# Six weight slots instead of four in the first stage of a hybrid trunk layer, with x loaded at once and PE's order rewritten

## The chip, the cores and the metric

One NeuronCore of one Trainium2 chip runs the whole layer as one program. The metric is the device time of one execution in microseconds (us). Times inside the profile count from the start of the profiled span. Engines are named as in the profile: PE is TensorE (PEld its weight loads), ACT ScalarE, DVE VectorE, POOL GpSimd and SP SyncE; "q" behind a name is the engine's sequencer, which issues DMAs.

## The reference

One inference step of a one-layer diffusion trunk in float32: 512 latent tokens and 128 context tokens, model width 2048. Only the beginning matters here:

```python
mod = silu(cvec) @ w_mod + b_mod                       # for c and c_ctx; w_mod is 2048 x 12288
sh1, sc1, g1, sh2, sc2, g2 = split(mod, 6)
h = rmsnorm(x, g_pre1) * (1 + sc1) + sh1
proj = h @ w_in
xr, gr, q, k, v, gates = split(proj, ...)              # v has 1024 columns
...
```

After that come a bidirectional recurrent branch, differential attention, an output projection and a mixture of 16 experts. The outputs are both token sets, the new key and value caches and the recurrent state.

## The kernel before

The program is written by hand: each engine has one list of instructions, and semaphores tie the lists together. Every float32 weight is split into a high and a low part (ACT writes `w_hi`, DVE `w_lo`), and a product is three matmuls, low x high, high x low, high x high (`three`, lines 540 to 544).

**The first stage** computes shift and scale (the first 4096 columns of `w_mod`), normalises and transposes x, and begins the values v with `w_in`. Its weights come in units of 1 MiB, each two DMAs of 512 KB on SP's queue (line 592) into one of four slots of `raw`. `START` (lines 69 to 73) lists the units: 32 units `("mod", m)` of `w_mod` and four units `("v", h)` of `w_in`. In this text unit i is the one at place i of the list, from 0. Before, v0 to v3 are units 8, 13, 22 and 31, and mod 31 is unit 35. Four more units for the second half of the values follow as units 36 to 39. `start_load` (line 583) issues unit i into slot i % 4 when the unit four places earlier has been used: a mod unit by PE (`start_used`), a v unit by DVE's low split (`lo_ready`). SP's list is in order, so a load that waits holds back all behind it.

**PE's list** (lines 2309 to 2393) is an order written out by hand from these pieces:
- `mod_unit(m)` (L2282): four matmuls of one unit against the columns of silu(c). Units 4s to 4s + 3 make row s; rows 0, 2, 4, 6 are shift quarters, rows 1, 3, 5, 7 scale quarters.
- `turn_x(t)` (L2271): 16 matmuls that transpose and scale tile t of x (five tiles of 128 tokens) into PSUM banks 4 to 7. It waits for the diagonal of 1/rms that DVE makes (`norm_diagonal`) from ACT's sum of squares (`square`), and for the copies of tile t - 1 out of the same banks (`take_x`, two by ACT, two by DVE).
- `turn_rows(s)` (L2295): turns row s, which ACT has copied from PSUM (`row_out`, L1047), into columns.
- `turn_parameters` (L2299): turns small parameter rows into PSUM.
- `first_values(k)` (L542 to L544): 15 matmuls of the first 512 value columns for block k of the model width. It needs `tokens(k)` and, for k = 0, 4, 8, 12, the split v unit. With `amid=s` a `turn_rows(s)` stands inside, behind six of the 15 matmuls.

**ACT and DVE** work h = 0 to 3 in order: split v unit h (for h = 0 ahead of the loop), copy or add rows 2h and 2h + 1 (`row_out`, `mod_columns`), then `tokens` for four blocks: ACT scales, shifts and takes the high part (L1037, L1040), DVE the low part (L1517). `tokens` of group h need A1 (L1511), which DVE writes after `turn_rows(2h + 1)`. So ACT splits v unit h only behind the tokens of group h - 1 (lines 1064 to 1072, 1543 to 1553):

```python
for h in range(4):
    if h:
        v_split_hi(act, h, 0); v_split_hi(act, h, 1)
        row_out(2 * h); row_out(2 * h + 1)
    act.wait_ge(S["a1_ready"], h + 1)
    for k in range(4 * h, 4 * h + 4):
        tokens(k)
```

After the last group ACT and DVE split unit 36, DVE computes a softplus in a dozen short steps (lines 1564 to 1592) and copies the values out of PSUM (`take_values`, L1541); PE's next stage, `wide(Q_V + 1, ...)`, waits for those copies.

**x** is loaded by ACT's own queue (`load_x`, L1016): tiles 0 and 1 behind silu(c), tile t + 2 behind `square(t)`. Small parameter rows come on POOL's queue. `mod_raw` (three slots of 8 KB a partition) is used only in the stage behind, where DVE computes the other modulation columns; before that its first slot holds `c2` and `sel2`, its third the diagonals.

Of the kernel before, what the change touches and what calls it, by code (L numbers as in the profile page):

```python
# [22 lines left out]
P = 128  # L23
D = 2048
# [25 lines left out]
NSLOT = 8  # L50
UNITS = 24
QUADS = [8, 2, 8, 8, 4, 8, NE * 6]
# [20 lines left out]
assert all(i % NRAW == m for m, i in V_AT.items()) and len(START) == (Q_V + 1) * NRAW  # L73
# [41 lines left out]
def trunk(nc, a, out_ctx, out_lat, out_k, out_v, out_state):  # L115
    ctx = ExitStack()
    with ctx:
# [42 lines left out]
        def place(at0, items):  # L160

            o, made = at0, {}
            for name, shape, dt in items:
# [21 lines left out]
        A["diag"] = at("diag", [P, 2, P], F32, mod_at + 2 * UB + 256)  # L185
# [246 lines left out]
        def f_loaded(t):  # L432

            j = (F_UNIT + t) % NSLOT
            return raw_loaded[j], (Q_EXP * INC if j < NRAW else 0) + (UNITS // NSLOT * NE + 1) * 16

# [9 lines left out]
        def exp_loads(e, k):  # L446

            return (Q_EXP * INC if k % NSLOT < NRAW else 0) + (UNITS // NSLOT * e + k // NSLOT + 1) * 16

# [22 lines left out]

        def start_loaded(eng, i):

            eng.wait_ge(raw_loaded[i % NRAW], (i // NRAW + 1) * INC)
# [86 lines left out]
        def _(sp):  # L562
# [7 lines left out]
            def wide(w, j, kq, c0):  # L570

                v = raw[:, j, :].rearrange("p (k n) -> p k n", k=4)
# [10 lines left out]
            def start_load(i, parts):  # L583

                if i >= NRAW:
                    what, n = START[i - NRAW]
# [4 lines left out]
                for dst, src in parts:  # L591
                    sp.dma_start(dst, src).then_inc(raw_loaded[i % NRAW], INC // 2)

            for i, (what, n) in enumerate(START):
                if what == "mod":
                    start_load(i, wide(w_mod, i % NRAW, n % 4, n // 4 % 2 * D + n // 8 * 512))
# [402 lines left out]
        def _(act):  # L999
# [6 lines left out]
            act.dma_start(ident[:], a["ident"]).then_inc(S["c_loaded"], 16)  # L1006
            act.wait_ge(S["const_set"], 1)
# [6 lines left out]
            def load_x(t):  # L1014
                src = a["x_sample"][0][t * P:(t + 1) * P, :] if t < TT - 1 else a["x_prompt"][0]
                act.dma_start(x_in[:, t, :], src).then_inc(x_loaded[t % 2], 16)  # L1016

            def square(t):

                act.wait_ge(x_loaded[t % 2], (t // 2 + 1) * 16)  # L1020
# [1845 lines left out]
```

## Time and profile before

| | us |
|---|---|
| median of 3 runs | 2847.84 |
| lowest, highest | 2847.01, 2848.12 |
| the profiled execution | 2848.99 |
| its span | 2847.4 |

A profile shows one execution. Rows with "busy" give the time in which an engine had an instruction running; matmuls overlap, so a busy PE need not be at its peak. A wait names the engine and the line whose work ended last before the waiting instruction went on. "DMA share" is the mean busy share of the core's 16 DMA engines (it can exceed 1, as packets overlap), GB/s what they moved, PEclk the granted clock of TensorE as a share of 2.4 GHz. q1 is SP's DMA queue, q10 ACT's, q0 POOL's.

### The profile page before, as it was taken

The page shows a single profiled execution, that of the slowest core. Times are in us where ns is not written, and L with a number is a line of the kernel's source. Part 1 is how long each engine was busy: PE and PEld are TensorE (multiplying, and loading weights), DVE is VectorE, ACT ScalarE, POOL GpSimd, SP SyncE. Part 2 cuts the span into 40 slices and gives each one's busy share as a digit, 9 for nine tenths or more (in the row PEclk, how much of TensorE's full clock was granted, in tenths as well). Part 3 has the DMA queues.
Part 4 walks back from the last instruction along what each step waited for, and adds up shares of the span by engine and source line. Part 5 has one row for each costly group of instructions (what it writes and reads, how often), then busy time and mean ns, then how long its engine had stood idle before and what let it go on. Part 6 is the DMA issues. An engine that isn't in the chain of part 4 may idle for free.

```text
span 2847.4 us, 40931 instructions
## 1 busy us (share of the span) xinstructions
PE 2791.4 (98%) x15008; PEld 2390.7 (84%) x15008; DVE 2106.8 (74%) x1918; ACT 1502.7 (53%) x1466; POOL 282.0 (10%) x337
## 2 busy tenths in 40 slices
PE   7999999999999999999999997999999999999998
PEld 5688888899999999999988776888888888888886
DVE  2339788796777777763344577888888888888888
ACT  4411221125556566552233455777777777777776
POOL 1000000002111111100000001001010101100100
PEclk9999999999999999999999997999999999999999
DMA  9877667664343443364343767999999999999997
GB/s 370 311 266 255 228 252 265 224 227 135 120 123 119 123 123 123 102 207 124 123 143 119 292 215 276 356 402 395 395 398 389 396 393 397 391 388 387 392 394 297
DMA packets 258406, 757.23 MB, mean 266 GB/s; under 512 B 20249, under 2 KB 127297, under 8 KB 194001
## 3 DMA queue, kind: packets, MB, share of 16 engines
q1 hardware_dynamic: 234272, 650.01, 61.3%
q0 software_dynamic: 23120, 100.71, 10.9%
q10 hardware_dynamic: 928, 5.33, 0.5%
q8 instruction: 59, 0.97, 0.1%
q14 instruction: 27, 0.21, 0.0%
HBM read 700.61 MB, written 55.37 MB: 265 GB/s over the span
## 4 chain that ended last, share of the span: by engine, by line
PE 91%; DVE 3%; DMA 2%; ACT 1%; issue 1%; DVEq 0%; ACTq 0%; SPq 0%; POOL 0%; POOLq 0%
PE ps L542 21%; PE ps L544 21%; PE ps L543 21%; PE ps L2402 5%; PE ps L2403 5%; PE ps L2404 5%; PE ps L2569 3%; PE ps L2571 3%; PE ps L2570 3%; PE ps L2259 2%; PE ps L2507 1%; DMA raw<-in_w_mod 1%; DVE rsd L1827 1%; PE ps L2282 1%; DVE xc L1649 0%
## 5 line engine op out<-in xcount | busy, mean ns | idle before, releaser
L467 DVE TENSOR_TENSOR we_lo<-raw,we_hi 128x2048 fp32r<-128x2048 f32 x384 | 877.5, 2290 | 114.0 <-ACT we_hi L462 113.8
L462 ACT ACTIVATE we_hi<-raw 128x2048 fp32r<-128x2048 f32 x384 | 736.9, 1920 | 261.4 <-PE ps L544 261.4
L411 ACT ACTIVATE w_hi<-raw 128x2048 fp32r<-128x2048 f32 x115 | 220.1, 1914 | 444.3 <-PE ps L544 356.5
L421 DVE TENSOR_TENSOR w_lo<-raw,w_hi 128x2048 fp32r<-128x2048 f32 x115 | 263.5, 2291 | 192.4 <-ACT w_hi L411 187.8
L542 PE MATMUL ps<-we_hi,xs_lo 128*128 128x512 f32 x1024 | 399.7, 390 | 0.1
L544 PE MATMUL ps<-we_hi,xs_hi 128*128 128x512 f32 x1024 | 399.3, 390 | 0.0
L543 PE MATMUL ps<-we_lo,xs_hi 128*128 128x512 f32 x1024 | 399.3, 390 | 0.0
L2402 PE MATMUL ps<-hi,w_lo 128*128 128x320 f32 x1152 | 365.3, 317 | 0.9 <-ACT stage L1122 0.9
L2403 PE MATMUL ps<-lo,w_hi 128*128 128x320 f32 x1152 | 355.9, 309 | 0.0
L2404 PE MATMUL ps<-hi,w_hi 128*128 128x320 f32 x1152 | 355.8, 309 | 0.0
L1614 DVE SCALAR_TENSOR_TENSOR mod_acc<-mod_raw,sc,mod_acc 128x2048 f32<-128x2048 f32 x120 | 276.7, 2348 | 3.3
L542 PEld LDWEIGHTS ps<-we_hi,xs_lo 128*128 128x128 f32 x1024 | 192.8, 188 | 41.9 <-issue 0.7
L544 PEld LDWEIGHTS ps<-we_hi,xs_hi 128*128 128x128 f32 x1024 | 192.8, 188 | 40.2
L543 PEld LDWEIGHTS ps<-we_lo,xs_hi 128*128 128x128 f32 x1024 | 192.8, 188 | 39.4
L2402 PEld LDWEIGHTS ps<-hi,w_lo 128*128 128x128 f32 x1152 | 216.3, 188 | 9.8 <-issue 8.9
L2403 PEld LDWEIGHTS ps<-lo,w_hi 128*128 128x128 f32 x1152 | 216.6, 188 | 0.0
L2404 PEld LDWEIGHTS ps<-hi,w_hi 128*128 128x128 f32 x1152 | 216.3, 188 | 0.0
L542 PE MATMUL ps<-we_hi,hid_lo 128*128 128x512 f32 x512 | 201.3, 393 | 0.4 <-DVE hid_lo L2166 0.4
L544 PE MATMUL ps<-we_hi,hid_hi 128*128 128x512 f32 x512 | 199.5, 390 | 0.0
L543 PE MATMUL ps<-we_lo,hid_hi 128*128 128x512 f32 x512 | 199.3, 389 | 0.0
L542 PE MATMUL ps<-hi,w_lo 128*128 128x512 f32 x448 | 175.2, 391 | 0.0
L544 PE MATMUL ps<-hi,w_hi 128*128 128x512 f32 x448 | 174.5, 389 | 0.0
(447 smaller groups left out, 4772.0 us busy)
## 6 DMA issues: line engine op xcount, KB each, us to landing
raw<-in_w_e_gate SPq DMA_DIRECT2D x128, 1024.0 KB, 8.0
raw<-in_w_e_up SPq DMA_DIRECT2D x128, 1024.0 KB, 7.5
raw<-in_w_e_down SPq DMA_DIRECT2D x128, 1024.0 KB, 12.1
raw<-in_w_in SPq DMA_DIRECT2D x144, 512.0 KB, 5.7
mod_raw<-in_w_mod SPq DMA_DIRECT2D x64, 1024.0 KB, 5.3
raw<-in_w_mod SPq DMA_DIRECT2D x64, 512.0 KB, 7.6
raw<-in_w_o SPq DMA_DIRECT2D x64, 512.0 KB, 4.9
d_proj<-g_stage POOLq DMA_DIRECT2D x32, 320.0 KB, 2.4
```

The source lines that it names most:

```text
L411: act.activation(w_hi[:, j % NHL, s], raw[:, slot, s], ACT.Copy).then_inc(hi_ready, 1 if fine else 2)
L421: dve.tensor_tensor(w_lo[:, j % NHL, s], raw[:, slot, s], w_hi[:, j % NHL, s].bitcast(F32), ALU.subtract).then_inc(lo_ready, 1 if fine else 2)
L462: act.activation(we_hi[:, k % NEH, :], raw_slot(k), ACT.Copy).then_inc(hi_ready, 2)
L467: TTn(we_lo[:, k % NEH, :], raw_slot(k), we_hi[:, k % NEH, :].bitcast(F32), ALU.subtract).then_inc(lo_ready, 2)
L542: pe.matmul(out, s_lo, m_hi, start=start, stop=False)
L543: pe.matmul(out, s_hi, m_lo, start=False, stop=False)
L544: return pe.matmul(out, s_hi, m_hi, start=False, stop=stop)
L1614: last = STT(mod_acc[:, v, :], w, c, mod_acc[:, v, :], ALU.mult, ALU.add)
L2402: pe.matmul(out, wl, hi[:, k, ms], start=(k % 16 == 0), stop=False)
L2403: pe.matmul(out, wh, lo[:, k, ms], start=False, stop=False)
L2404: last = pe.matmul(out, wh, hi[:, k, ms], start=False, stop=(k == KT - 1))
L2569: pe.matmul(out, wl, hi[:, k, ms], start=(kk == 0), stop=False)
```

## The change

The first stage gets six slots: the four of `raw` and the second and third of `mod_raw` (`first_slot`), whose diagonals move to a spare tile. `START` becomes one list with v0 to v3 at places 6, 13, 20 and 27, so that each lies in slot h; `start_load` waits for the unit six places earlier. ACT issues all five tiles of x right behind the constants, each on a semaphore of its own (three are shared with later loads, whose targets rise by 16), and loads the table for Sqrt early. ACT, DVE and PE get new orders: PE starts with `turn_x(0)` and alternates it with units; `turn_rows(3)`, `(5)` and `(7)` no longer stand inside a `first_values`; `turn_parameters` writes to bank 3; `take_x` of all tiles now precedes the column copies on DVE and `row_out(0)` on ACT. `loads_ahead` replaces the count of earlier loads that the experts' slots expect.

```diff
@@ constants and START
+NFIRST = 6
-QUADS = [8, 2, 8, 8, 4, 8, NE * 6]
+QUADS = [5, 2, 8, 8, 4, 8, NE * 6]
-START = [("mod", m) for m in range(8)] + [("v", 0)] + [x for h in range(1, 4) for x in [
-    ("mod", 8 * h + m) for m in range(4)] + [("v", h)] + [("mod", 8 * h + m) for m in range(4, 8)]]
+V_PLACE = (6, 13, 20, 27)
+_mods = iter(range(32))
+START = [("v", V_PLACE.index(i)) if i in V_PLACE else ("mod", next(_mods)) for i in range(36)]
@@ SBUF
-        A["diag"] = at("diag", [P, 2, P], F32, mod_at + 2 * UB + 256)
+        A["diag"] = at("diag", [P, 2, P], F32, PLACED["spare"])
@@ semaphores and slots
+        x_sems = x_loaded + [S["g2_loaded"], S["vec_lat_loaded"], S["rope_loaded"]]
+        def first_slot(i):
+            j = i % NFIRST
+            return raw[:, j, :] if j < NRAW else mod_raw[:, j - NRAW + 1, :]
         def start_loaded(eng, i):
-            eng.wait_ge(raw_loaded[i % NRAW], (i // NRAW + 1) * INC)
+            eng.wait_ge(raw_loaded[i % NFIRST], (i // NFIRST + 1) * INC)
+        def loads_ahead(j):
+            return Q_EXP * INC if j < NRAW else (Q_V + 1) * INC if j < NFIRST else 0
@@ SP
             def start_load(i, parts):
-                if i >= NRAW:
-                    what, n = START[i - NRAW]
+                if i >= NFIRST:
+                    what, n = START[i - NFIRST]
...
-                    sp.dma_start(dst, src).then_inc(raw_loaded[i % NRAW], INC // 2)
+                    sp.dma_start(dst, src).then_inc(raw_loaded[i % NFIRST], INC // 2)
@@ ACT
             act.dma_start(ident[:], a["ident"]).then_inc(S["c_loaded"], 16)
+            for t in range(TT):
+                src = a["x_sample"][0][t * P:(t + 1) * P, :] if t < TT - 1 else a["x_prompt"][0]
+                act.dma_start(x_in[:, t, :], src).then_inc(x_sems[t], 16)
...
+            act.activation(misc[:, 6:7], eps_col, ACT.Sqrt)
...
-            load_x(0)
-            load_x(1)
             for t in range(TT):
                 square(t)
-                if t + 2 < TT:
-                    load_x(t + 2)
-                if t:
-                    take_x(t - 1)
+                if t >= 2:
+                    take_x(t - 2)
+            take_x(TT - 2)
+            take_x(TT - 1)
             row_out(0)
             v_split_hi(act, 0, 0)
             row_out(1)
             v_split_hi(act, 0, 1)
-            take_x(TT - 1)
@@ DVE
-            dve.wait_ge(S["rows_turned"], 2)
-            own.done(dve.tensor_copy(A["cols_b"][:], ps[:, 4, 0:48]))
-            own.done(dve.tensor_copy(A["cols2"][:], ps[:, 5, 0:105]))
-            own.settle()
             for t in range(TT):
                 norm_diagonal(t)
                 if t:
                     take_x(t - 1)
+            take_x(TT - 1)
+            dve.wait_ge(S["rows_turned"], 2)
+            own.done(dve.tensor_copy(A["cols_b"][:], ps[:, 3, 0:48]))
+            own.done(dve.tensor_copy(A["cols2"][:], ps[:, 3, 64:169]))
+            own.settle()
+            mod_columns(0)
             v_split_lo(dve, 0, 0)
-            mod_columns(0)
+            mod_columns(1)
             v_split_lo(dve, 0, 1)
-            take_x(TT - 1)
-            mod_columns(1)
@@ PE
             pe.wait_ge(S["c_ready"], 1)
+            turn_x(0)
             mod_unit(0)
+            turn_x(1)
             mod_unit(1)
+            turn_x(2)
+            mod_unit(2)
+            mod_unit(3)
+            turn_x(3)
             turn_parameters()
-            for m in range(2, 8):
-                mod_unit(m)
-                if m == 7:
-                    turn_rows(0)
-                if m >= 3:
-                    turn_x(m - 3)
+            mod_unit(4)
+            turn_x(4)
+            mod_unit(5)
+            mod_unit(6)
+            turn_rows(0)
+            mod_unit(7)
+            pe.wait_ge(S["xt_act"], 2 * TT)
+            pe.wait_ge(S["xt_dve"], 2 * TT)
+            mod_unit(8)
             turn_rows(1)
...
-            mod_units(8, 11)
+            mod_units(9, 11)
             first_values(0)
+            first_values(1)
             mod_units(11, 12)
-            first_values(1)
-            mod_units(12, 13)
             first_values(2)
+            mod_units(12, 14)
             turn_rows(2)
-            mod_units(13, 16)
-            first_values(3, amid=3)
-            mod_units(16, 18)
+            mod_units(14, 16)
+            first_values(3)
+            mod_units(16, 17)
+            turn_rows(3)
+            mod_units(17, 18)
             first_values(4)
-            mod_units(18, 20)
+            mod_units(18, 21)
             first_values(5)
-            mod_units(20, 21)
+            mod_units(21, 22)
+            turn_rows(4)
+            mod_units(22, 24)
             first_values(6)
-            turn_rows(4)
-            mod_units(21, 24)
-            first_values(7, amid=5)
-            mod_units(24, 26)
+            turn_rows(5)
+            first_values(7)
+            mod_units(24, 27)
             first_values(8)
-            mod_units(26, 28)
             first_values(9)
-            mod_units(28, 30)
             first_values(10)
+            mod_units(27, 30)
             turn_rows(6)
             mod_units(30, 32)
-            first_values(11, amid=7)
+            first_values(11)
+            turn_rows(7)
             for k in range(12, KT):
                 first_values(k)
```

## Rows read from the trace of the kernel before

**Rows 1.** Busy time by stretch; engines, then PEclk, DMA share, GB/s.
```profile
0.00:10.50 10.50, 0.31 (x1) 0.18 (x1) 2.11 (x9) 1.72 (x3) 8.61 (x18) 1.00 0.82 283
15.50:20.40 4.90, 0.00 (x0) 0.00 (x0) 0.00 (x0) 3.44 (x4) 0.00 (x0) 0.68 1.01 401
20.40:121.60 101.20, 96.99 (x628) 63.64 (x629) 30.11 (x50) 49.29 (x75) 0.00 (x0) 0.98 1.04 383
139.70:260.00 120.30, 120.29 (x533) 99.59 (x534) 70.97 (x40) 20.08 (x15) 6.30 (x10) 1.00 0.69 255
```

**Rows 2.** Waits of PE and SP's queue, 0 to 140: total, times, longest.
```profile
PE ps L2282 <- DMA raw<-in_w_mod: 8.9, 6, 5.0
...
SPq L592 <- PE ps L2282: 64.0, 21, 7.1
...
SPq L592 <- DVE w_lo L487: 11.3, 4, 3.8
```

**Rows 3.** The chain, 0 to 260: start, us, what.
```profile
38.01 3.77 PE ps L2271 x32
...
47.43 0.80 PE ps L2295 x8
...
55.30 0.99 PE ps L2282 x8
...
59.93 1.00 PE ps L2282 x8
...
95.65 0.79 PE ps L2295 x8
...
120.84 0.80 PE ps L2295 x8
...
139.71 0.47 PE ps L542
```

**Rows 4.** DMA queues from 13 to 19 us: packets, MB, share.
```profile
q10 hardware_dynamic: 258, 1.98, 80.0%
q1 hardware_dynamic: 256, 0.49, 21.8%
```

**Rows 5.** Timeline of ACT and its queue: x0's issue, its first square.
```profile
9.05 0.84 ACTq L1016 DMA_DIRECT2D x_in<-in_x_sample  x2
...
16.94 1.91 ACT L1022 ACTIVATE junk<-x_in 128x2048 f32<-128x2048 f32 x1 [7.74 <-DMA x_in<-in_x_sample]
```

**Rows 6.** Timeline of PE: the first turn_x.
```profile
22.31 4.65 PE L2271 MATMUL ps<-diag,x_in 128*128 128x128 f32 x32
```

**Rows 7.** Busy time by stretch again; DMA share and GB/s stand last.
```profile
66.00:74.00 8.00, 8.00 (x59) 4.43 (x51) 1.16 (x3) 3.67 (x7) 0.00 (x0) 1.00 0.95 315
100.00:103.00 3.00, 3.00 (x19) 2.14 (x12) 1.22 (x2) 2.97 (x5) 0.00 (x0) 1.00 1.05 365
103.00:117.00 14.00, 12.73 (x73) 7.53 (x72) 3.62 (x4) 3.90 (x6) 0.00 (x0) 1.00 1.05 387
```

**Rows 8.** Timeline of SP's queue: three units' issues.
```profile
46.09 0.89 SPq L592 DMA_DIRECT2D raw<-in_w_mod  x2
...
109.96 0.88 SPq L592 DMA_DIRECT2D raw<-in_w_mod  x2
...
133.87 0.88 SPq L567 DMA_DIRECT2D raw<-in_w_in  x2
```

**Rows 9.** DMA issues at 109.96 and 133.87: KB each, median us to landing.
```profile
raw<-in_w_mod SPq DMA_DIRECT2D x2, 512.0 KB, 6.1
...
raw<-in_w_in SPq DMA_DIRECT2D x2, 512.0 KB, 4.4
```

**Rows 10.** Timelines of ACT and DVE: tokens 8 to 11, then v3's split.
```profile
96.87 1.20 ACT L1037 ACTIVATE xT<-xT,cols,A 128x512 f32<-128x512 f32 x2 [2.15 <-DVE A L1511]
...
103.70 0.74 ACT L1040 ACTIVATE hi<-xT 128x640 fp32r<-128x640 f32 x1
...
106.48 2.01 ACT L481 ACTIVATE w_hi<-raw 128x1024 fp32r<-128x1024 f32 x2 [2.04 <-DMA raw<-in_w_in]
...
107.57 2.36 DVE L487 TENSOR_TENSOR w_lo<-raw,w_hi 128x1024 fp32r<-128x1024 f32 x2 [2.28 <-ACT w_hi L481]
```

More of the change, by code:

```diff
@@ L66 @@
 MOD_FROM = [sum(MOD_TILES[:n]) for n in range(8)]
-START = [("mod", m) for m in range(8)] + [("v", 0)] + [x for h in range(1, 4) for x in [
-    ("mod", 8 * h + m) for m in range(4)] + [("v", h)] + [("mod", 8 * h + m) for m in range(4, 8)]]
+V_PLACE = (6, 13, 20, 27)
+_mods = iter(range(32))
+START = [("v", V_PLACE.index(i)) if i in V_PLACE else ("mod", next(_mods)) for i in range(36)]
 MOD_AT = {m: i for i, (what, m) in enumerate(START) if what == "mod"}
 V_AT = {m: i for i, (what, m) in enumerate(START) if what == "v"}
-assert all(i % NRAW == m for m, i in V_AT.items()) and len(START) == (Q_V + 1) * NRAW
+assert all(i % NFIRST == m for m, i in V_AT.items()) and len(START) == (Q_V + 1) * NFIRST
 ORDER = (4, 2, 3, 0, 1)
@@ L591, in start_load @@
                 for dst, src in parts:
-                    sp.dma_start(dst, src).then_inc(raw_loaded[i % NRAW], INC // 2)
+                    sp.dma_start(dst, src).then_inc(raw_loaded[i % NFIRST], INC // 2)
             for i, (what, n) in enumerate(START):
                 if what == "mod":
-                    start_load(i, wide(w_mod, i % NRAW, n % 4, n // 4 % 2 * D + n // 8 * 512))
+                    start_load(i, wide(w_mod, i % NFIRST, n % 4, n // 4 % 2 * D + n // 8 * 512))
                 else:
@@ L2055, in _ @@
                 if c == 0:
-                    dve.wait_ge(S["vec_lat_loaded"], 32)
+                    dve.wait_ge(S["vec_lat_loaded"], 48)
                 if c == 2:
@@ L2215, in _ @@
             expert(NE - 1, 1, True)
-            dve.wait_ge(S["g2_loaded"], 32)
+            dve.wait_ge(S["g2_loaded"], 48)
             def gain(i, t):
@@ L2282, in mod_unit @@
                     last = pe.matmul(ps[32 * kk:32 * kk + 32, bank, :], c2[:, 4 * kp + kk, :],
-                                     raw[:, i % NRAW, kk * 512:kk * 512 + 512], start=(kp == 0), stop=(kp == 3))
+                                     first_slot(i)[:, kk * 512:kk * 512 + 512], start=(kp == 0), stop=(kp == 3))
                 last.then_inc(S["start_used"], 1)
@@ L2300, in turn_parameters @@
                 pe.wait_ge(par_loaded, N_PAR * 16)
-                turn(ps[:, 4, 0:48], A["rows3"][:], 48)
-                turn(ps[:, 5, 0:105], A["rows2"][:], 105).then_inc(S["rows_turned"], 1)
+                turn(ps[:, 3, 0:48], A["rows3"][:], 48)
+                turn(ps[:, 3, 64:169], A["rows2"][:], 105).then_inc(S["rows_turned"], 1)
             def spread_lambda():
@@ L2340, in wide, with first_values @@
                     last.then_inc(halves_used, 2)
-            def first_values(k, amid=None):
+            def first_values(k):
                 kq, s = k // 4, slice(k % 4 * 512, k % 4 * 512 + 512)
@@ L2353, in first_values @@
                         last.then_inc(S["bank_done"], 1)
-                    if amid is not None and t == 1:
-                        turn_rows(amid)
                 if k % 4 == 3:
```

15 lines of the change are left out of this document (5 added, 10 removed).

## Prediction

> **What bounds the kernel now.** The page comes first: PE is busy nearly throughout, and the change touches only the first 5% of the span. The table by stretch shows what that part can pay [rows 1]: from 139.7 us on PE has no gap (120.29 of 120.30 us), so only the moment counts at which it enters that stage. Ahead of it PE stands still for 4.9 us (15.5 to 20.4), and from 20.4 to 121.6 us it is busy for 96.99 of 101.20 us while the DMA share is 1.04. Both limits lie on top of each other. The waits say how [rows 2]: PE waited 8.9 us for w_mod, but SyncE stood 64.0 us in front of a slot that PE had not released and 11.3 us in front of one that VectorE's low split had not. With four slots the transfers run on PE's releases and PE on the transfers. The chain runs accordingly through pieces of PE and pieces of w_mod up to the last turn_rows (L2295), which ends at 120.84 + 0.80 = 121.6 us [rows 3].
>
> Behind that turn_rows the order is fixed and the same in both kernels: VectorE writes A1, ScalarE and VectorE make tokens 12 to 15, split the next unit, walk the softplus chain and copy v_stage, and PE enters the next stage at 139.7, 18.1 us after turn_rows(7) ended [rows 3]. I call that end R7. **The change moves the end of the kernel by what it moves R7**, as nothing later is edited but semaphore targets that count x's tiles in.
>
> **x's five tiles at once.** Queue shares are read from 13 to 19 us [rows 4]: ScalarE's queue took 1.98 MB and SyncE's 0.49 MB, four to one. x0 was issued at 9.05 and squared from 16.94 [rows 5], 7.9 us. Issued behind the constants at about 2.5 it lands near 10.4; the tiles behind it follow 3.2 us apart (1.05 MB at 1.98 MB per 6 us), x2 near 16.8. Total bytes are unchanged, so for the last weights this part is worth nothing: the same queues carry 41 MiB. The early Sqrt costs nothing, its table load falls into the wait for x0, 7.74 us long before [rows 5]; the five issues (0.4 us each) lie where ScalarE waited for cols_ready.
>
> **PE up to turn_rows(1).** PE now starts with turn_x(0), which needs x0 squared (2.1 us), rooted and put on the diagonal (0.9): 13.5 us instead of 10.5. turn_x(0) took 4.65 us in the stretch after a stand of 4.9 us with a granted clock of 0.68, that is partly at 1.2 instead of 2.4 GHz [rows 1, 6]; warm ones take 3.77 [rows 3]. I take 4.65, since PE starts from a stand here too, with 3.77 and 5.5 (another such surcharge) as ends. Then mod_unit(0) 1.0; turn_x(1) waits for ScalarE's copy, which is now queued behind square(2): 16.8 + 2.4 + 0.6 = 19.8; four more turn_x 15.1, six units 5.7, the parameters 0.4, turn_rows(0) 0.9: 41.9; mod_unit(7) to 42.9. mod_unit(8) is the tenth unit, so 15 MiB with x: 2.8 us of start (10.5 us at 283 instead of 387 GB/s, [rows 1]) plus 15 x 2.71 us (1 MiB at 387 GB/s, [rows 7]) plus 0.6 to report, 44.0. It ends at 44.9, turn_rows(1) at **45.8**. Before, it ended at 48.2 [rows 3], so 2.4 us are won here.
>
> **Six slots, and who holds them.** Releases by PE are no longer late: after 45.8 us every ordinary unit is asked for over 5 us ahead. But SyncE's queue is in order, and units 12, 19, 26 and 33 each wait until VectorE has split the V unit six places earlier. Two of these are late.
> Unit 12 waits for v0's second half, which now stands behind mod_columns(1): 45.8 + 0.4 + 1.2 = 47.4, when unit 11 is almost through. The old unit 12 was issued at 46.09 [rows 8], so the lead is gone here. On an empty queue a unit is home 5.2 us after its first issue (133.87, median 4.4 us, the second half later, [rows 8, 9]); with work ahead it took 7.0 (109.96 and 6.1, [rows 8, 9]). Restarting a dry queue costs extra: 1.5 us in 66 to 74 us (315 instead of 387 GB/s), 0.2 us in 100 to 103 [rows 7]; I take 0.8, between them. Unit 12 lands at 53.4.
> From there 14 units at 2.71 bring mod 23 (unit 26) at 91.3. Its slot is free in time: mod 15 lands at 66.9, turn_rows(3) ends 6.4 later (a unit, first_values(3), a unit, the turn) and v2 is split 11.4 behind that, at 84.7, when unit 25 is still 3.9 us from home. Mod 23 takes 0.9, first_values(6) 3.6 (4.63 for a unit and a first_values between 55.30 and 59.93, [rows 3]), turn_rows(5) 0.9: that ends at **96.8**, called R5; before 96.4 [rows 3].
> Unit 33 waits for v3, which ScalarE may split only behind tokens 8 to 11. From R5: A1 0.4, tokens 7.6 (96.87 to 104.44), split 2.0, VectorE's last half 1.4 behind it [rows 10]: 11.4, so 108.2. The units up to 32 are home at 91.3 + 6 x 2.71 = 107.6: the queue is dry again. Unit 33 lands 5.2 + 0.8 later, mod 31 two units on, 119.6 (before: about 117.1, by the issue at 109.96). Old v3 was the 32nd unit and blocked one load; new v3 is the 28th and blocks three.
>
> **The tail.** first_values(11) now stands whole (3.6) ahead of turn_rows(7), where six of its fifteen products did: mod 31 0.9 + 3.6 + 0.9 = 5.5. R7 = 119.6 + 5.5 = **125.1** against 121.6: **+3.5 us**. PE alone, never waiting, would need 27.3 from R5 (five first_values 18.2, eight units 7.3, two turn_rows 1.8): 124.1, one microsecond less, so the transfer decides. Behind R7 PE has nothing left to do until tokens 12 are there, 3.2 us, but VectorE's chain of 18.1 us is as long as before and covers it. In one line R7 = R5 + 28.3. Parameters in bank 3, the moved column copies (0.5 us) and the moved diagonal lie ahead of turn_rows(0) and cost nothing while x's copies take longer.
>
> The sum is made against the profiled execution, 2848.99 us with a span of 2847.4; the median of the three runs shown is 2847.84, so +3.5 gives **2851.3 us**. Without restart costs it is +1.9, with 1.5 us for each +4.9; the clock of turn_x(0) adds 0.9 either way: +1.0 to +5.8.
>
> The pace of 387 GB/s is that of 103 to 117 us [rows 7]. The Trainium skill (DMA: Bandwidth & Descriptors, Specifications) gives an HBM limit of about 358 GB/s for a core. An estimate from that page's figure makes a unit 2.93 us, the sixteen units on the path 3.5 us longer and the sum +7.0; the trace disagrees, and its 387 decides.
>
> **Rivals.** *The supply keeps ahead.* For: 75 us of slot waits are what six slots are made for. If unit 12 comes without a gap, R5 is near 94.6 and R7 near 122.0 to 122.9, about +0.8, 2848.6. If unit 33 also came without one, mod 31 would land at 2.8 + 41 x 2.71 + 0.6 = 114.5 and R7 at 120.0: -1.6, 2846.2. Against: the order of tokens and splits on ScalarE ties unit 33 to R5 + 11.4. Chance 0.17.
> *The dry queue costs more*, the slower side: at units 12 and 33 the load takes 7.0 as with a full queue and 1.5 us of restart, 2.5 more at each place: +8.5, 2856.3. It decides from R5 at 99.0 on. For: the 66 to 74 stretch and the 6.1 us landing [rows 7, 9]; against: the empty queue's 4.4. Chance 0.20.
> *A slower pace throughout*, the 365 GB/s of 100 to 103 us [rows 7]: 2.87 a unit, sixteen units on the path, 2.6 more, +6.1, 2853.9. Against it the longer row with 387. Chance 0.02. This is the side on which the Trainium skill's limit of 358 GB/s (same page and section) lies.
> *A gain of over 5.7 us* would need mod 31 home by 110, before 41 MiB can pass at 387 GB/s; 0.03, for what I overlook.
>
> **Numbers.** My forecast has 0.58. A measurement of this kernel tells about 0.2%, 5.7 us, from no change. Slower by more: 0.22, the second and third rivals. Faster by more: 0.03. Within: 0.75. The range goes from 2846.0, the first rival's far end, to 2856.0, most of the second; up to 0.2 is left out.
>
> **What would show it.** Right: x0 squared before 11 us; turn_rows(1) ending near 46; SyncE's longest waits in the stage on L487, with issues near 47 and 108; bytes below 387 GB/s just behind both; turn_rows(5) near 97; the last turn_rows ending at 124 to 127, PE idle about 3 us behind it; the next stage shifted whole. Wrong: no gap in the transfers near 108, or the last turn_rows before 122.

## The result and the profile after

The kernel after takes 2856.18 us (median), the kernel before 2847.84: a ratio of 1.0029, 95% interval 1.0021 to 1.0037, so 8.3 us slower. That is above the 0.2% that a measurement of this kernel tells from no change. The profiled execution of after was a long one, 2858.92 us with a span of 2857.3, 9.9 above the span of before.

The stretches of after, as [rows 1] and [rows 7]: engines as there, then PEclk, DMA share and GB/s.

```profile
14.31:20.50 6.19, 6.19 (x36) 6.07 (x40) 1.14 (x3) 4.90 (x7) 0.00 (x0) 1.00 1.03 414
...
78.26:83.50 5.24, 5.24 (x12) 4.11 (x13) 2.28 (x3) 5.14 (x9) 0.00 (x0) 0.50 1.05 386
119.90:130.85 10.95, 9.29 (x39) 5.51 (x39) 0.00 (x0) 0.60 (x1) 0.00 (x0) 0.69 1.05 387
134.26:138.00 3.74, 3.74 (x11) 2.98 (x12) 1.65 (x2) 3.68 (x7) 0.00 (x0) 0.65 0.00 0
149.97:260.00 110.03, 110.03 (x486) 91.13 (x486) 59.94 (x34) 18.48 (x14) 5.52 (x9) 1.00 0.66 243
...
48.50:51.50 3.00, 1.37 (x12) 0.20 (x8) 1.07 (x3) 2.94 (x6) 0.00 (x0) 0.75 0.61 165
108.82:115.89 7.07, 7.07 (x34) 5.59 (x32) 1.80 (x2) 0.35 (x1) 0.00 (x0) 1.00 0.60 197
```

Read the row of 149.97 first: from there on PE is busy without a gap, as it was from 139.71 [rows 1]. PE enters that stage 10.3 us later and the span is 9.9 longer, so all but some tenths of the difference arises ahead of that moment. The two rows at the bottom are the queue running dry: 165 and 197 GB/s where the rows around them have 386 and 387. And three rows have a granted clock of 0.50 to 0.69, so PE was at the lower of its two levels, 1.2 GHz, for all or part of them; in [rows 1] the stretch from 20.4 to 121.6 had 0.98.

The waits of after, 0 to 140, for [rows 2]: total, times, longest.

```profile
PE ps L2281 <- DVE diag L1501: 6.3, 1, 6.3
...
PE ps L554 <- DVE lo L1527: 5.8, 2, 3.4
...
PE ps L2292 <- DMA mod_raw<-in_w_mod: 4.2, 4, 1.7
...
SPq L604 <- DVE w_lo L499: 24.0, 3, 11.7
SPq L604 <- PE ps L2292: 22.8, 13, 3.9
```

SyncE's 64.0 us in front of PE have become 22.8, as two more slots should make them. Its wait for VectorE's low split has grown from 11.3 to 24.0, three waits in place of four, each long (5.9, 6.4 and 11.7 us, ahead of units 12, 26 and 33). PE's wait for tokens (L554 waits for `lo`) has grown from 1.4 to 5.8 us, once 2.4 and once 3.4.

The chain of after from turn_rows(5) to the products for block 12, as [rows 3]: start, us, what.

```profile
98.49 0.80 PE ps L2305 x8
...
99.52 0.18 DVE A L1521
...
107.18 1.05 ACT w_hi L493
108.26 2.37 DVE w_lo L499 x2
110.65 0.37 SPq L604
...
113.17 9.40 DMA mod_raw<-in_w_mod
...
122.62 1.93 PE ps L2292 x8
124.55 0.73 PE ps L554
125.28 0.43 PE ps L555
...
129.15 0.23 PE ps L556
...
130.06 0.80 PE ps L2305 x8
...
132.52 0.74 ACT hi L1053
133.29 0.84 DVE lo L1527
...
134.26 0.47 PE ps L554
```

This is the forecast's path, link by link: turn_rows(5), A1, tokens, v3's split, SyncE's issue, the loads, mod 31, first_values(11), turn_rows(7). What it adds is the width of the products: 0.43 us each up to 128.3, then 0.23.

### The profile page after: what moved, and what is told of

It is laid out like the page before. It is cut to its first block, busy times and chain, and to the rows that moved or that the text cites. A ratio compares the mean times of both kernels' runs of the same rounds, so it can differ in the third digit from the quotient of the medians.

```text
span 2857.3 us, 40974 instructions
## 1 busy us (share of the span) xinstructions
PE 2796.8 (98%) x15008; PEld 2396.2 (84%) x15008; DVE 2106.6 (74%) x1918; ACT 1502.0 (53%) x1467; POOL 285.7 (10%) x337
## 4 chain that ended last, share of the span: by engine, by line
PE 92%; DVE 3%; ACT 2%; DMA 2%; issue 1%; ACTq 0%; DVEq 0%; SPq 0%; POOL 0%; POOLq 0%
PE ps L554 21%; PE ps L556 21%; PE ps L555 21%; PE ps L2420 5%; PE ps L2421 5%; PE ps L2422 5%; PE ps L2587 3%; PE ps L2588 3%; PE ps L2589 3%; PE ps L2269 2%; PE ps L2525 1%; DVE rsd L1837 1%; PE ps L2281 1%; PE ps L2292 1%; DMA mod_raw<-in_w_mod 1%
## 5 line engine op out<-in xcount | busy, mean ns | idle before, releaser
L554 PE MATMUL ps<-we_hi,xs_lo 128*128 128x512 f32 x1024 | 399.4, 390 | 0.8 <-DVE xs_lo L2137 0.8
L554 PEld LDWEIGHTS ps<-we_hi,xs_lo 128*128 128x128 f32 x1024 | 192.6, 188 | 42.2 <-issue 1.3
L554 PE MATMUL ps<-we_hi,hid_lo 128*128 128x512 f32 x512 | 201.4, 393 | 0.4 <-DVE hid_lo L2176 0.4
L554 PE MATMUL ps<-hi,w_lo 128*128 128x512 f32 x448 | 175.2, 391 | 0.0
```

Source lines behind the costliest of these rows:

```text
L554: pe.matmul(out, s_lo, m_hi, start=start, stop=False)
```

## The experiments

Times are medians; a ratio is always to the kernel before, measured beside each group on the same chip (its medians were 2847.76 to 2848.58). "Spread" is the start of the two small products ahead of the next stage (L2316 in after), the last landmark that all kernels share. The last three columns come from the one profiled execution of each kernel, which lies up to 3.7 us from its median (2860.14 against 2856.47). Edits are shown shortened, with several calls on one line.

| kernel | us | ratio, interval | turn_rows(5) ends | turn_rows(7) ends | spread |
|---|---|---|---|---|---|
| before | 2847.84 | | 96.4 | 121.6 | 138.84 |
| after | 2856.18 | 1.0029, 1.0021 to 1.0037 | 99.3 | 130.9 | 149.66 |
| after, again | 2856.78 | 1.0030, 1.0018 to 1.0042 | 98.6 | 127.2 | 147.16 |
| turns 3, 5, 7 inside | 2849.72 | 1.0009, 1.0000 to 1.0018 | 96.8 | 123.6 | 140.80 |
| turn 7 inside | 2853.16 | 1.0020, 1.0011 to 1.0028 | 98.6 | 125.3 | 142.54 |
| v3 last | 2855.41 | 1.0025, 1.0014 to 1.0036 | 99.5 | 126.2 | 146.22 |
| v3 last, turn 7 inside | 2850.49 | 1.0008, 0.9999 to 1.0017 | 99.8 | 124.4 | 141.57 |
| v2, v3 later | 2858.33 | 1.0039, 1.0026 to 1.0053 | 102.6 | 129.2 | 149.25 |
| PE kept turning | 2857.11 | 1.0032, 1.0020 to 1.0044 | 98.9 | 127.8 | 145.03 |
| turning, fitted | 2856.47 | 1.0027, 1.0017 to 1.0037 | 101.2 | 131.1 | 148.36 |
| slots alone | 2853.53 | 1.0023, 1.0014 to 1.0032 | 99.8 | 128.7 | 145.95 |
| x alone | 2855.06 | 1.0024, 1.0014 to 1.0034 | 106.0 | 130.2 | 147.43 |
| after with old x | 2865.65 | 1.0063, 1.0050 to 1.0077 | 109.0 | 139.0 | 157.70 |
| v0 early | 2857.26 | 1.0032, 1.0019 to 1.0044 | 98.2 | 128.2 | 146.77 |
| all mended | 2848.79 | 1.0003, 0.9994 to 1.0012 | 96.7 | 121.3 | 138.52 |
| all mended, no turning | 2849.61 | 1.0004, 0.9995 to 1.0013 | 96.8 | 121.4 | 138.64 |
| all mended, v0 early | 2846.52 | 0.9994, 0.9985 to 1.0003 | 96.5 | 121.1 | 138.27 |
| best order | 2846.14 | 0.9993, 0.9984 to 1.0002 | 95.3 | 119.9 | 137.15 |
| best order, no turning | 2846.36 | 0.9992, 0.9983 to 1.0001 | 95.8 | 120.4 | 137.64 |

### The turns of rows

```diff
-            first_values(3); mod_units(16, 17); turn_rows(3); mod_units(17, 18)
+            first_values(3, amid=3); mod_units(16, 18)
-            first_values(6); turn_rows(5)
+            first_values(6, amid=5)
-            first_values(11); turn_rows(7)
+            first_values(11, amid=7)
```

> The kernel after, with turn_rows(3), (5) and (7) put back inside first_values(3), (6) and (11), behind the sixth of their fifteen products, as in the kernel before. Theory (the new order on PE makes each turn of rows late, each late turn makes a V split and with it a load late, and PE then stands and goes on at half clock): turn_rows(5) ends about 96 us instead of 99.3, unit 33 is issued near 107.5 instead of 110.65, mod 31 lands near 119.5, turn_rows(7) ends near 123 instead of 130.85, no stand of PE ahead of first_values(4); time 2848 to 2850 us, 6 to 8 below the kernel after. Rival (the supply of weights sets the end and the order on PE hides behind it): turn_rows(7) still at 129 to 131, time 2855 to 2857 us.

The theory held: 2849.72 us, turn_rows(5) at 96.8, v3's split done and unit 33 issued at 108.15, turn_rows(7) at 123.6. Three turns that come nine products earlier give back 6.5 of the 8.3 us. The last of them alone:

```diff
-            first_values(11); turn_rows(7)
+            first_values(11, amid=7)
```

> The kernel after, with turn_rows(7) alone put back inside first_values(11), behind the sixth of its fifteen products. Loads and all before mod 31 stay. Theory (the nine products that stood ahead of the turn are on the path, at half clock for the most part): turn_rows(7) ends near 128 instead of 130.85, the nine products then run in the wait for tokens 12 and PE is at full clock for first_values(12); the next stage enters about 4 us earlier, time 2852 to 2853 us. Rival (the end of turn_rows(7) does not set the end of the kernel): it ends as early, and the time stays at 2855 to 2857 us.

Timeline of PE in that kernel: start, us, line, in brackets the idle time before and what ended it.

```profile
121.89 1.07 PE L2292 MATMUL ps<-mod_raw,c 128*32 128x512 f32 x8 [1.73 <-DMA mod_raw<-in_w_mod]
124.39 0.95 PE L2305 MATMUL ps<-sel,m_rows 128*128 128x2 f32 x8
128.75 0.47 PE L554 MATMUL ps<-w_hi,lo 128*128 128x512 f32 x1 [1.21 <-DVE lo L1527]
```

2853.16 us, 3.0 below after, a little less than expected (turn_rows(7) ended at 125.3, where 128 was expected). Two things happen. The nine products (2.1 us at full clock) leave the path to the turn, and they lie in the wait for tokens 12, which shrinks from 3.41 to 1.21 us (1.22 in before). PE then runs blocks 12 to 15 at full clock: from the end of the turn to the spread it is 17.2 us, as in before, and not 18.8 and 20.0 as in the two executions of after.

### The places of the V units

```diff
-V_PLACE = (6, 13, 20, 27)
+V_PLACE = (6, 13, 26, 33)
```

> The kernel after, with the four V units at places 6, 13, 26, 33 of the order of loads instead of 6, 13, 20, 27. Unit 33 is then v3 itself and waits for nothing but v2's split, and no unit behind it waits for v3. Theory (the restart of a dry queue behind v3's split costs the last weights 5 us): no gap in the transfers near 108 us, mod 31 lands near 117 to 118 instead of 122.6, turn_rows(7) ends near 126, time 2850 to 2852.5 us. Rival (the end is set by PE's order and clock, not by the last loads): turn_rows(7) at 129.5 or later, time 2855 to 2858 us.

A miss, 2858.33 us. Waits of PE in that kernel, 80 to 130:

```profile
PE ps L2305 <- ACT m_rows L1060: 2.8, 1, 2.8
PE ps L554 <- DVE lo L1527: 2.4, 1, 2.4
```

Unit 33 was issued at 107.14, now behind a slot that PE had not released (SyncE stood 6.0 us), and the queue still ran dry for two microseconds (102 and 119 GB/s from 107 to 109). But no load came too late for PE: from turn_rows(5) to turn_rows(7) it needed 26.6 us without one wait, against 31.6 and 28.6 in the two executions of after. However, turn_rows(5) came 3.3 later: ScalarE works in order, v2 now lands later, and the copy of the rows for turn_rows(4) stands behind its split. One wait was taken away and another made. So v3 alone:

```diff
-V_PLACE = (6, 13, 20, 27)
+V_PLACE = (6, 13, 20, 33)
```

> The kernel after, with v3 at place 33 of the order of loads instead of 27, v0 to v2 where they are. No load up to mod 31 then waits for v3's split, and v2 is not later (it was in the run with v2 at place 26, where ScalarE's copy of the rows for turn_rows(4) stood behind v2's split). Theory (the dry queue behind v3's split costs the end about 5 us): turn_rows(5) stays near 99.3, mod 31 lands near 117.7 instead of 122.6, PE never waits from there and turn_rows(7) ends 26.6 behind turn_rows(5), near 126; time 2850.5 to 2853 us. Rival (PE gets no further for it, another wait takes its place): turn_rows(7) at 129 or later, time 2855 us or more.

```profile
125.20 0.95 PE L2305 MATMUL ps<-sel,m_rows 128*128 128x2 f32 x8
129.55 0.77 PE L554 MATMUL ps<-w_hi,lo 128*128 128x512 f32 x1 [3.41 <-DVE lo L1527]
```

Timeline of PE: the last turn and block 12. The steps were as expected (turn_rows(5) 99.5, turn_rows(7) 126.15, no wait for mod 31 any more), the time was not: 2855.41 us, only 0.8 below after. From turn_rows(5) to turn_rows(7) PE's own work takes 26.6 us, so against the 28.6 of the second execution of after there were 2 us to win at most; and behind the turn PE stands for 3.41 us as there, then needs 16.7 us for the four blocks instead of 13.8. Hence both edits together:

```diff
-V_PLACE = (6, 13, 20, 27)
+V_PLACE = (6, 13, 20, 33)
-            first_values(11); turn_rows(7)
+            first_values(11, amid=7)
```

> The kernel after with two edits together that were run apart: v3 at place 33, and turn_rows(7) inside first_values(11). Theory (each alone leaves the other bound: with v3 last PE's own work sets the end, with the turn inside the last weights do): mod 31 lands near 117.5, turn_rows(7) ends 24.4 behind turn_rows(5), near 123.5, PE at full clock for first_values(12); time 2849 to 2851 us, more than the two gains of 0.8 and 3.0 us added. Rival (the gains only add up or overlap): 2852 us or more.

2850.49 us, 5.7 below after and 6.3 below its repetition, more than 0.8 and 3.0 added; but the excess of 1.9 to 2.5 us lies within the intervals. In the rows the gains add up: from the end of turn_rows(5) to the spread it is 48.6 us in after, again, 46.7 with v3 last, 43.9 with the turn inside and 41.8 with both. **The edits take away two parts of one path**: PE's wait for mod 31 (1.58 us in after, again, 1.73 with the turn inside, none with v3 last), and the products ahead of turn_rows(7) with the half clock behind it. That one part hides the other is not shown.

### TensorE's clock

```diff
+            def idle_turns(bank, n):
+                for _ in range(n):
+                    turn(ps[:, bank, 0:P], ident[:])
+            idle_turns(3, 40)          # ahead of turn_x(0); likewise 6, 15, 20, 15, 30 in later waits
```

> The kernel after, with idle transposes of the identity on PE in its waits: 40 ahead of turn_x(0), 6 and 15 around mod 9, 20 ahead of first_values(4), 15 ahead of mod 31, 30 ahead of first_values(12); their results go to banks that are written over. Nothing else is moved, so loads, splits and order stay. Theory (of the 9.2 us by which turn_rows(7) ends later, some 4 to 5 are work of PE at half clock behind its waits): turn_x(0) 4 to 5 us instead of 6.2, first_values(4) and first_values(11) 3.6 to 4.0 instead of 6.4 and 5.4, turn_rows(7) near 127.5, time 2850 to 2852 us. Rival (the half clock falls into time that the supply of weights sets anyway): the products are as fast, but turn_rows(7) moves by less than 1.5 us and the time is 2854.5 to 2857 us.

The rows obeyed the theory, the time the rival: turn_x(0) took 3.76 us, turn_rows(7) ended at 127.8, and the median was 2857.11. With fewer transposes, beside the unchanged kernel:

> The kernel after with idle transposes in PE's waits as in the run that kept PE turning, but fewer of them, so that none delays the work behind it: 36 ahead of turn_x(0), 4 and 12 around mod 9, 18 ahead of first_values(4), 13 ahead of mod 31, 26 ahead of first_values(12). Theory (the half clock costs the kernel after 2 to 4 us; the first such run gave that back by transposes that were too many): turn_rows(7) ends near 127.5, time 2 to 4 us below the unchanged kernel of the same chip. Rival (the half clock costs the median execution nothing, the supply of weights sets it): time within 1 us of the unchanged kernel.

> The kernel after, unchanged, on the chip of the run with idle transposes fitted to the waits, as its measure. Its profiled execution so far was the longest of eleven, 2858.9 us against a median of 2856.2. Theory (how long PE stays at half clock behind a wait differs between executions of the same kernel): other granted clocks in the same stretches, and with them a turn_rows(7) off by 1 us or more from 130.85; median 2855 to 2857.5 us. Rival (the half clock is the same each time): turn_rows(7) within 0.5 us of 130.85.

2856.47 and 2856.78 us: again no gain. The kernel after, again, in stretches of its own, for the stretches 119.90:130.85 and 134.26:138.00 above:

```profile
119.02:127.15 8.13, 6.54 (x40) 4.10 (x39) 0.17 (x1) 0.60 (x1) 0.00 (x0) 1.00 1.05 388
130.55:135.00 4.45, 4.45 (x11) 3.48 (x12) 1.65 (x2) 4.35 (x8) 0.00 (x0) 0.50 0.03 10
```

So the same kernel had mod 31 and first_values(11) at full clock in this execution and mostly at half clock in the other, and turn_rows(7) ended 3.7 us apart. And the fitted transposes, in stretches:

```profile
71.47:77.00 5.53, 5.53 (x23) 4.22 (x23) 0.00 (x0) 0.60 (x1) 0.00 (x0) 0.65 1.05 387
82.36:86.00 3.64, 3.64 (x19) 2.77 (x23) 1.65 (x2) 3.58 (x7) 0.00 (x0) 1.00 1.05 388
```

There first_values(4) was at full clock, as meant, but PE had to wait 1.65 us for a unit ahead of first_values(3), to 69.6 (in after PE had it by 68.3 without a wait), and that block ran at 0.65 instead. So in this execution PE's waits were in other places, not fewer; why that unit came later no run separates. One part is the same in every profiled execution of the kernels with the new order: where PE stands for 3.41 us behind turn_rows(7), the spread follows 18.6 to 20.1 us behind the turn (both executions of after and four other kernels); where it has products or transposes there, 17.2. So the half clock is real in the rows and costs 1.4 to 2.9 us of the stage. That it costs the median as much is not shown: both kernels with transposes have that stretch back and are no faster.

### The parts alone

Six slots and the new places of the V units, with `first_slot`, `loads_ahead` and the moved diagonals, in the kernel before:

```diff
+NFIRST = 6
+V_PLACE = (6, 13, 20, 27)
-                if i >= NRAW:
-                    what, n = START[i - NRAW]
+                if i >= NFIRST:
+                    what, n = START[i - NFIRST]
```

> The kernel before, with six weight slots and the four V units at places 6, 13, 20, 27 as in the kernel after, but with x loaded as before and the order on PE, ScalarE and VectorE as before. Theory (two more slots alone neither win nor lose, since the transfers already run at 387 GB/s; the loss is the order's): turn_rows(7) ends 121 to 123 us, time within 2 us of the kernel before. Rival (the places of the V units in six slots make the queue dry whatever the order): unit 33 again issued behind v3's split, turn_rows(7) at 126 or later, time 2852 us or more.

x at once, in the kernel before, with the early Sqrt:

```diff
+            for t in range(TT):
+                act.dma_start(x_in[:, t, :], src).then_inc(x_sems[t], 16)
-            load_x(0)
-            load_x(1)
-                if t + 2 < TT:
-                    load_x(t + 2)
```

> The kernel before, with x's five tiles issued at once by ScalarE behind the constants, the early Sqrt and the semaphores that go with it; four slots and the old order on PE. Theory (x's packets take most of the transfers from 7 to 23 us, as behind the change, so that the first weights come late, and the old order, which begins with four mod units, stands in front of them): units 2 and 3 land near 25 and 27.5 us instead of 12.9 and 20.4, turn_x(0) starts near 28.5 instead of 22.3, turn_rows(1) ends 52 to 54 instead of 48.2, time 2851 to 2854 us. Rival (the bytes are the same, so the order in which they come costs nothing later): turn_rows(7) within 1 us of 121.6, time 2847 to 2849 us.

And the kernel after with those lines the other way round:

> The kernel after with x's tiles issued as in the kernel before (two behind the columns, one more behind each square); six slots and the new order on PE stay. Theory (the new order begins with turn_x(0), so it needs x early; the earlier x is worth what the new order would else lose at its start): turn_x(0) starts near 20.5 instead of 14.5, turn_rows(1) ends near 51 instead of 47.2, unit 12 comes 3 us later, time 2858 to 2861 us. Rival (as x alone on the old order cost 7 us, x early costs here too, and the first weights that come sooner make up for it): turn_rows(5) at or below 99.3 and 2856 us or less.

Slots alone 2853.53 us (the rival was right), x alone 2855.06, somewhat worse than the theory said, and without the early x 2865.65, 9 above after and 4.6 above the theory's upper end. PE in the kernel with x alone:

```profile
14.81 1.94 PE L2280 MATMUL ps<-raw,c 128*32 128x512 f32 x8 [2.37 <-DMA raw<-in_w_mod]
...
24.97 1.94 PE L2280 MATMUL ps<-raw,c 128*32 128x512 f32 x8 [6.90 <-DMA raw<-in_w_mod]
...
54.67 0.95 PE L2293 MATMUL ps<-sel,m_rows 128*128 128x2 f32 x8
```

The third unit is there at 24.97 and the fourth at 27.68, where before PE had them at 14.40 and 20.45; the first transpose of x starts at 29.5 instead of 22.3, and turn_rows(1) ends at 55.6 instead of 48.2. In after with the old x the reverse holds: turn_x(0) starts at 19.54 behind a wait of 11.13 us. The early x and an order that begins with x belong together; either without the other costs 7 and 9 us. In the kernel with slots alone PE waits 2.60 us for a unit at 39.65 (0.45 us in before), the next turn_x takes 5.93 us, turn_rows(1) ends at 53.9 and unit 12 is issued at 51.34; from there it goes as in after.

The queues of after from 13 to 19 us, as [rows 4]:

```profile
q10 hardware_dynamic: 268, 1.93, 79.1%
q1 hardware_dynamic: 267, 0.51, 22.5%
```

While x is on its way the weights get a fifth of the engines, before as after; what matters is which of the two PE needs first. Both queues moved almost the same number of packets (268 and 267; 258 and 256 before), about 7.2 KB each for x and 1.9 KB for the weights, so the four to one in bytes goes with the size of the packets. The Trainium skill (DMA: Bandwidth & Descriptors, Issuing engines are not separate DMA queues) says that transfers issued by different engines share the same DMA engines and that the choice saves issue time alone. The rows agree on the sharing; the 7 and 9 us show that it still matters when x is issued, since the weights of that time get the smaller share.

### v0's split, and what beats the kernel after

```diff
-            row_out(1)
             v_split_hi(act, 0, 1)
+            row_out(1)
-            mod_columns(1)
             v_split_lo(dve, 0, 1)
+            mod_columns(1)
```

> The kernel after, with the second half of v0's split ahead of the rows of turn_rows(1) on ScalarE and ahead of mod_columns(1) on VectorE, so that unit 12's slot is free some 2 us earlier. Theory (the queue runs dry at unit 12 as well, and that is what still lies between the mended kernels and an earlier turn_rows(5)): unit 12 issued near 46.3 instead of 48.7, before unit 11 is home; unit 14 lands near 58.6 instead of 59.6; unit 26 near 91.5 instead of 92.7 to 93; turn_rows(5) 1 to 1.5 us earlier, time 2854 to 2855.5 us. Rival (PE, not unit 26, sets turn_rows(5) here): unit 26 is earlier but turn_rows(5) moves by less than 0.5, time 2855.7 to 2857.5 us.

2857.26 us, the rival's time, though unit 26 did not come earlier as the rival said. Unit 12 was issued at 46.11, before unit 11 was home, but SyncE then stood longer at unit 26, in the waits of SP's queue from 75 to 95:

```profile
SPq L604 <- DVE w_lo L499: 7.6, 1, 7.6
```

It was issued at 86.36, no earlier than in after (86.20), and now the queue ran dry there (144 GB/s from 86 to 88, 386 in after). Weights that come sooner wait for v2's split, which hangs on turn_rows(3). The mended kernels take these ties away together: turns 3 and 7 inside, v3 at place 33, first_values(5) ahead of mod 18, first_values(6) ahead of mod 22, turn_rows(5) right behind mod 23, with idle transposes ahead of turn_x(0) and around mod 9, and without:

```diff
+            first_values(3, amid=3); mod_units(16, 18); first_values(4)
+            first_values(5); mod_units(18, 22); turn_rows(4)
+            first_values(6); mod_units(22, 24); turn_rows(5)
```

> The kernel after with all that the runs so far point to: turns of rows 3 and 7 inside first_values(3) and (11), v3 at place 33, idle transposes ahead of turn_x(0) and around mod 9, first_values(5) ahead of mod 18, first_values(6) ahead of mod 22, turn_rows(5) right behind mod 23. Theory (three causes: late turns, v3's split ahead of the last loads, half clock behind waits): turn_rows(5) ends near 96.5, mod 31 lands near 117.7, turn_rows(7) ends 121.5 to 122.5; time 2847 to 2849 us, level with the kernel before. Rival (something else in the change costs some us as well, which none of these edits touches): 2850 us or more.

> The run with all mended, without its idle transposes ahead of turn_x(0) and around mod 9. Theory (behind the first stop PE has little to wait for, and the supply sets mod 23 and mod 31 in any case): turn_x(0) near 6 us again and first_values(0) partly at half clock, but turn_rows(5) still near 96.7 and turn_rows(7) 121.3 to 122.5; time 2848.5 to 2850 us. Rival (the clock of the first 60 us is what made that run level with the kernel before): 2851 us or more.

Both as the theory had them, 2848.79 and 2849.61 us, level with the kernel before. With v0's earlier split on top:

> The run with all mended, idle transposes included, with the same earlier split of v0. There turn_rows(5) follows mod 23 at once and nothing else is late. Theory (the supply sets it): unit 26 near 91.5 instead of 92.85, mod 31 near 116 instead of 117.2, turn_rows(7) ends 120 to 120.7 instead of 121.3, time 2847 to 2848.2 us, at or just below the kernel before. Rival (turn_rows(7) is set by PE's work, and the tail behind it is fixed): turn_rows(7) at 121 or later, time 2848.3 to 2849.5 us.

2846.52 us: 2.3 below the kernel without it, below the theory's range even, but turn_rows(7) came at 121.1, where the rival had it, and moved by only 0.2 us; the two intervals overlap, so a gain by this edit is not shown. Last, first_values(6) from behind turn_rows(4) to ahead of mod 21:

```diff
-            mod_units(18, 22); turn_rows(4); first_values(6)
+            mod_units(18, 21); first_values(6); mod_units(21, 22); turn_rows(4)
```

> The run with all mended and v0 split earlier, with first_values(6) moved from behind turn_rows(4) to ahead of mod 21, where PE waited 1.35 us and PE's work behind mod 23 gets shorter. Theory (with both dry queues gone, PE's own work behind turn_rows(5), 24.6 us, sets turn_rows(7), so an earlier turn_rows(5) comes through until mod 31's landing near 115.4 stops it): turn_rows(5) ends near 94 instead of 96.5, turn_rows(7) near 119 instead of 121.07, time 2844 to 2846 us, below the kernel before (about 2848). Rival (another wait takes its place, tokens 8 or a row copy): turn_rows(7) at 120.5 or later, time 2846.5 us or more.

> The same without any idle transposes on PE. Theory (from mod 23 on the supply sets the pace, and the clock of the first 60 us hides behind it): turn_x(0) near 6 us and first_values(0) partly at half clock again, turn_rows(5) within 1.5 us of the run with idle transposes, time at most 1.5 us above it, 2844.5 to 2847 us. Rival (with nothing else late, the half clock behind the first waits is on the path): turn_rows(7) 2 us or more later than with them, 2847 us or more.

PE in the kernel with the best order:

```profile
94.25 1.05 PE L2309 MATMUL ps<-sel,m_rows 128*128 128x2 f32 x8 [0.72 <-ACT m_rows L1060]
...
118.98 0.95 PE L2309 MATMUL ps<-sel,m_rows 128*128 128x2 f32 x8
123.34 0.47 PE L554 MATMUL ps<-w_hi,lo 128*128 128x512 f32 x1 [1.26 <-DVE lo L1527]
...
137.98 0.47 PE L554 MATMUL ps<-w_hi,lo 128*128 128x512 f32 x1 [0.46 <-DVE v_stage L1551]
```

turn_rows(7) ends 1.7 us earlier than in before and the next stage begins 1.7 us earlier (137.98 against 139.71); the times are 2846.14 and 2846.36 us, both 1.9 to 2.1 below the kernel before of the same chip (2848.27). The expected 119 for turn_rows(7) was 0.9 too hopeful and the time sits at the edge between theory and rival. Three kernels at 0.9992 to 0.9994 point the same way, but each interval still holds 1, so "probably 2 us faster" is all that can be said.

## Why the prediction was wrong

The forecast was +3.5 us, less than a measurement of this kernel tells from no change; it came out at +8.3. Its range missed by 0.2 us.

**Right, step by step.** x0 was squared from 11.31 (said: lands 10.4). SyncE's longest waits are the V splits, with issues at 48.69 and 110.65 (47.4 and 108.2); the third, unit 26 at 86.20, was said to be free at 84.7 and left the queue full (386 to 387 GB/s from 84 to 92). v3's split was done 11.4 us behind turn_rows(5), to a tenth, in both executions of after (99.28 to 110.65, 98.56 to 109.93). mod 31 started 12.0 and 11.7 us behind that issue, said was 11.4. In the second execution mod 31, first_values(11) and the turn took 5.5 us as worked out (121.67 to 127.15). The pace behind it all was 386 to 388 GB/s. That was taken from a row against the limit of 358 GB/s; the Trainium skill elsewhere (Perfetto Trace Analysis, Roofline) calls 358 a core's share when both cores of a pair draw on the memory and says that one core alone can pull more, which these rows bear out.

**The first step that failed: the landing of mod_unit(8), "2.8 us of start" plus "15 x 2.71 us" plus "0.6 to report, 44.0".** In after PE stood for it and started it at 45.07; turn_rows(1) ended at 47.1 instead of 45.8 and unit 12 was issued 1.3 late. Timeline of PE in after, and the DMA queue of the weights there from 0 to 44.5, 0.6 ahead of that start:

```profile
45.07 1.06 PE L2292 MATMUL ps<-raw,c 128*32 128x512 f32 x8 [0.39 <-DMA raw<-in_w_mod]
...
q1 hardware_dynamic: 5728, 11.05, 68.0%
```

The ten units up to mod 8 are 10.49 MB. The other 0.56 MB, 1.4 us at 387 GB/s by estimate, belong to units behind, which the sum left out; the start itself cost less than its 2.8 us (16.49 MB had moved in all, 42.6 us at that pace, which leaves 1.9). That this is the cause is read from the bytes and not tested.

"I take 4.65" for turn_x(0), with 3.77 and 5.5 as ends, was too low as well: it took 6.19 and 6.66 us and began at 14.31 and 14.55 instead of 13.5. But this is not what made the path late, and the 0.9 us that the sum gave its clock either way were not on the path. In the five kernels with transposes ahead of it turn_x(0) took 3.74 to 3.81 us, turn_rows(1) ended at 46.9 to 47.5 all the same, and PE stood longer for mod 8 instead, as in the kernel that kept PE turning:

```profile
14.62 3.76 PE L2285 MATMUL ps<-diag,x_in 128*128 128x128 f32 x32
...
45.48 1.07 PE L2296 MATMUL ps<-raw,c 128*32 128x512 f32 x8 [1.19 <-DMA raw<-in_w_mod]
```

From there the delay is handed on. In the second execution PE waits for mod 23 and starts it at 93.08, 44.3 us behind unit 12's issue at 48.80; said was 43.9. So turn_rows(5) ended at 98.6 instead of 96.8. (With v0 early unit 12 was issued 2.7 us earlier and mod 23 came only 0.4 earlier, at 92.71: then v2's split sets it.) In the first execution it ended at 99.3; there PE did not wait for mod 23 and came late itself, behind the block that ran at half clock from 78.26.

**The second, and the larger in the repetition: "VectorE's chain of 18.1 us is as long as before and covers it".** From the end of turn_rows(7) to the spread it took 17.2 us in before and in every kernel with the turn inside first_values(11), and 18.8 and 20.0 in the two executions of after. The wait of 3.41 us was seen (3.2), and tokens 12 come no later behind the turn than in before. But in before nine products lay in that wait, PE stood for 1.22 us and went on at a granted clock of 1.00; now it stands for all of it and goes on at 0.50 and 0.65 (rows above), so its 60 products end behind VectorE. The sum priced the longer stop as a wait that is covered and left out the clock behind it. Turning inside first_values(11) again, which takes 2.1 us off the path as well, gave back 3.0 us.

Summed for the second execution: 1.8 from turn_rows(5), 0.3 from the loads, 2.8 from the tail, on top of +3.5: 8.4 at the spread, where its row has 147.16 - 138.84 = 8.3. In the first execution mod 31, first_values(11) and the turn took 8.2 us instead of 5.5, at a granted clock of 0.69.

**A part mis-priced rather than a term:** "for the last weights this part is worth nothing" holds of x only together with the new order; each without the other costs 7 to 9 us.

**The rivals.** *The dry queue costs more* named almost the time, 2856.3, by a mechanism that did not occur: it wanted loads of 7.0 us and 1.5 of restart, while unit 33's two halves had a median of 4.4 us to landing and the step from issue to mod 31 exceeded the forecast by 0.3 to 0.6. Its trigger (turn_rows(5) at 99.0 or later) was met in one execution only. *The supply keeps ahead* fell on the waits. But its condition was one worth having: with the turns inside, v3 last and v0 early, the queue does not run dry up to mod 31 (387 GB/s from 52 to 112), PE never waits for mod 31, and the change is no longer slower.

**What stays open** is how much of the 8.3 us the half clock makes in a median execution. It tells two executions of one kernel apart, and transposes took it out of the rows of the tail, but not out of the time; the part of the span behind the spread, untouched by all edits, varied from 2706.1 to 2710.2 us between kernels, so single profiles cannot decide on 2 us.

## What to carry to other kernels

More buffers move the wait to the next owner of a slot: ask who releases each slot last (here a split behind tokens behind a turn of rows), since in an ordered queue that one holds all loads behind it. A turn or copy that others wait for belongs inside the block of work around it, not behind it; the rest of the block then lies in the wait that the turn starts. And where single edits are worth hardly more than the intervals (0.8 and 3.0 us here, 5.7 together), follow their parts of the path in the rows, too: the medians alone tell neither that they add up nor that they hide each other.

## What the runs showed of the hardware

- PE's granted clock was 0.50 from 78.26 to 83.50, behind a stop of 2.41 us, and 0.69 over a stretch with stops of 0.25 and 1.66 us, but 1.00 over the same work in another execution, with a stop of 1.58. The Trainium skill (TensorE: Matmul & The Clock Gate, What you observe and What's actually happening) describes half rate as the state at rest that activity lifts, with a turning point that moves from run to run; the rows agree on both.
- turn_x(0) took 6.19 us in a stretch whose granted clock reads 1.00, and 3.74 to 3.81 us where transposes on PE ran ahead of it. The duration and the clock row do not fit, so the row alone doesn't tell the pace there.
- Around the two dry places the core moved 165 GB/s for 3 us and 197 for 7; the first loads behind them had medians of 4.6 and 4.4 us to landing, less than the 6.1 of a load with work ahead of it [rows 9].
